# Token sets of 256 and 264 columns, side by side in PSUM, in a hybrid decoder layer

## The chip, the cores and the metric

The kernel runs on one core of a Trainium2 chip. The metric is the device time of one execution in microseconds (us). TensorE does the matrix products, VectorE and ScalarE the elementwise work, GpSimd a few set-up steps and the DMA requests for cached keys. PSUM, into which TensorE writes its products, has 8 banks; in this kernel it is the tensor `PS[128, 8, 512]` of float32, so a bank holds 512 columns.

## The reference

One layer of a decoder whose heads stand in parallel: eight attention heads with forget gates, and eight blocks of a gated linear recurrence. There are 512 new prompt tokens (one sequence) and 8 sample tokens, one for each of eight sequences with 2048 cached positions. All 520 tokens go through the same weights:

```
xn = rms_norm(x, g_mix)                       # 520 tokens x 2048
z  = xn @ w_in                                # q | k | v | forget | lru x | lru gate, 5 x 1024 + 8 columns
att = forgetting attention over z's q, k, v (prompt: causal; samples: 2048 cached rows + the new one)
lru = gelu(gate) * rg_lru(causal_conv(x-branch))
x  = x + concat(rms_norm(att), rms_norm(lru)) @ w_out         # 2048 x 2048
x  = x + square(relu(rms_norm(x, g_ffn) @ w_up)) @ w_down     # 2048 -> 8192 -> 2048
y  = rms_norm(x, g_final)
```

The new keys, values, forget logs, convolution rows and recurrent states are returned too. Everything is float32.

## The kernel before

**Layout.** Features lie on the 128 partitions and tokens along the free dimension: `A[128, 16, 520]` holds 16 feature tiles of all T = 520 tokens (512 prompt tokens, then the 8 samples).

**Precision.** TensorE's float32r form is the cheaper and the less exact of its two float forms. So each operand is split in a high and a low part (`XH`/`XL` or `HH`/`HL` for activations, `WH`/`WL` for weights), and each product is three: high x high, low x high, high x low. ScalarE makes the high parts of the weights and VectorE the low ones.

**Tiles.** A product tile is 128 output features x 520 tokens. 520 columns don't fit in a bank, so the tile takes a pair of banks and the tokens two sets, c = 0 and c = 1, with HT = T // 2 = 260 columns each. Bank 2p holds tokens 0 to 259 of pair p in its columns 0 to 259; bank 2p + 1 holds tokens 260 to 519 in its columns 0 to 259. The function `products` issues, for every contraction tile k, six matmuls: (xh, wh) for c = 0, 1, (xl, wh) for c = 0, 1, (xh, wl) for c = 0, 1. `pair_view(p)` is what other engines read of a pair: two runs of 260 columns, 512 apart.

**Stages around the change.** `unit` makes a tile of the input projection (16 k, 96 matmuls) and of the first hidden features. Units alternate between bank pairs 0 and 1 (`at`, `tile_wait`): while TensorE fills one pair, ScalarE or VectorE copies the other and then increments `tile_out`. Attention, recurrence, and the sums over cached values use banks 4 to 7 and are inserted between a unit's matmuls by hand (`insert`). `out_products` does the same for w_out with 8 k and 48 matmuls a tile. `down_tile` (4 k, 24 matmuls) makes the tiles of w_down; there the four pairs take turns, and `add_rows` on VectorE adds a finished pair to `A` and increments `d_out`.

**The up products** (`up_pair`, lines L2488 to L2490) work on one token half of 260 columns at a time, in a seven-product scheme whose operands are sums and differences of the two halves. They, the last four tiles of w_down in the last round (`split_products`), and the sums of squares (`norm_sums`) write columns 0 to 259 of single banks.

**Copies of one head.** For the keys and the values, `rows_out` copies tokens 0 to 259 (L947), tokens 260 to 511 (L948) and the 8 samples (L949) from three places; for the convolution input, L1002, L1003 and L1004 do the same. Other copies read `pair_view` in one instruction: L804, L848 and the gelu of L1025 on ScalarE, L1699 (`add_heads`), L1831 (`add_rows`) and L1905 (`scaled_tile`) on VectorE.

Of the kernel before, what the change touches and what calls it, by code (L numbers as in the profile page):

```python
# [9 lines left out]
ALU = mybir.AluOpType  # L10
ACT = mybir.ActivationFunctionType
# [8 lines left out]
def hymba_step(nc, x_prompt, x_sample, cache_k, cache_v, cache_logf, state_conv, state_h, page_table,  # L20
# [76 lines left out]
    with ExitStack() as ctx:  # L97
# [232 lines left out]
        def one(i):  # L330
            return bass.ds(i, 1)
# [88 lines left out]
        def pair_view(pair):  # L420

            return PS[:, 2 * pair:2 * pair + 2, 0:HT]
# [339 lines left out]
        def _(act):  # L762
# [33 lines left out]
            def lru_tile(u, m):  # L796

                k = out_tile(u, m)
                slot = tile_wait(U_O + 2 * u + m, 0)
                act.wait_ge(xl_ready, KD + (k + NH) % KD + 1)  # L800
                act.wait_ge(nsq_ready, (k + NH) % KD + 1)
                if k < NH:
                    act.wait_ge(queries_saved, 1)
                nc.scalar.activation(A[:, k, :].rearrange("p (c t) -> p c t", c=2), pair_view(slot), ACT.Copy)\  # L804
                    .then_inc(tile_out[slot], 1)
# [40 lines left out]
            def query_out(n, half, k):  # L846
                slot = tile_wait(n, half)
                nc.scalar.activation(A[:, one(k), :].rearrange("p a (c t) -> p (a c) t", c=2),  # L848
                                     pair_view(slot), ACT.Copy).then_inc(tile_out[slot], 1)
# [95 lines left out]
            def rows_out(full, dst, samples, i):  # L945

                nc.scalar.activation(dst[:, 0:HT], PS[:, 2 * full, 0:HT], ACT.Copy)  # L947
                nc.scalar.activation(dst[:, HT:SEQ], PS[:, 2 * full + 1, 0:HB], ACT.Copy)  # L948
                nc.scalar.activation(samples[:, one(i), :].rearrange("p a b -> p (a b)"), PS[:, 2 * full + 1, HB:HT], ACT.Copy)\  # L949
                    .then_inc(tile_out[full], 1)  # L950

            def step(i, head, prev, older=True, final=False):
# [44 lines left out]
                if head:  # L997
                    slot = tile_wait(U_L + 2, 2 * i)
                    if prev:
                        act.wait_ge(lru_done, i)  # L1000
                    W3 = CW - 1
                    nc.scalar.activation(XW[:, W3:W3 + HT], PS[:, 2 * slot, 0:HT], ACT.Copy)  # L1002
                    nc.scalar.activation(XW[:, W3 + HT:W3 + SEQ], PS[:, 2 * slot + 1, 0:HB], ACT.Copy)  # L1003
                    nc.scalar.activation(XW[:, W3 + SEQ:].rearrange("p (b j) -> p b j", j=CW)[:, :, W3],  # L1004
                                         PS[:, 2 * slot + 1, HB:HT], ACT.Copy).then_inc(tile_out[slot], 1)
# [19 lines left out]
                    nc.scalar.activation(PT[:, T:2 * T].rearrange("p (a t) -> p a t", a=2), pair_view(slot),  # L1025
                                         ACT.Gelu_apprx_tanh).then_inc(tile_out[slot], 1)
# [249 lines left out]
        def _(dve):  # L1276
# [418 lines left out]
            def add_heads(u):  # L1695

                for m, tmp_t in enumerate((TA, TB)):
                    slot = tile_wait(U_O + KD + 2 * u + m, 0)
                    V.tensor_tensor(tmp_t.rearrange("p (c t) -> p c t", c=2), pair_view(slot), RSA.rearrange("p (c t) -> p c t", c=2),  # L1699
                                    ALU.mult).then_inc(tile_out[slot], 1)  # L1700
# [202 lines left out]
            def scaled_tile(n):  # L1903
                slot = tile_wait(T_F + n, 0)
                V.scalar_tensor_tensor(hf[:, n, :].rearrange("p (a t) -> p a t", a=2), pair_view(slot), 0.0,  # L1905
                                       RS[:, :].rearrange("p (a t) -> p a t", a=2), ALU.max, ALU.mult).then_inc(tile_out[slot], 1)
# [107 lines left out]
        def _(pe):  # L2014
            mm = nc.tensor.matmul

            def products(xh, xl, wh, wl, dsts, kts, insert={}, first=True, last=True, ready=None):

                for n, k in enumerate(kts):
                    if ready and n in ready:
                        pe.wait_ge(*ready[n])
                    for x in (xh, xl):
                        for c in range(2):
                            mm(dsts[c], wh(k), x[:, k, c * HT:(c + 1) * HT], start=first and n == 0 and x is xh, stop=False)  # L2026
                    for f in insert.get(2 * n, ()):
# [8 lines left out]
            def unit(n, half, tile, tile_half, insert={}, kts=range(KD), first=True, last=True, ready=None, halves=False):  # L2036
# [11 lines left out]
                ins = products(XH, XL, lambda k: WH[slot][:, k * P:(k + 1) * P], lambda k: WL[slot][:, k * P:(k + 1) * P],  # L2048
                               [PS[:, 2 * pair + c, 0:HT] for c in range(2)], kts, insert, first, last, ready)
# [6 lines left out]
            def out_products(u, m, kts, insert={}, ready=None):  # L2056
# [4 lines left out]
                if kts[0] == k0:  # L2061
# [4 lines left out]
                               [PS[:, 2 * pair + c, 0:HT] for c in range(2)], kts, insert, kts[0] == k0, last, ready)  # L2066
# [426 lines left out]
            def down_tile(c, d, m, pair, kts, rows={}):  # L2493
# [3 lines left out]
                                [PS[:, 2 * pair + c2, 0:HT] for c2 in range(2)], kts, insert=rows, first=kts[0] == 0, last=kts[-1] == CF - 1)  # L2497
# [167 lines left out]
```

## Time and profile before

| | us |
|---|---|
| median of 3 runs | 2259.0 (2258.14 to 2259.13) |
| the profiled execution | 2259.51 |
| its span, first to last instruction | 2257.6 |
| TensorE busy | 2232.6 |
| VectorE busy | 1609.0 |
| ScalarE busy | 854.2 |
| GpSimd busy | 155.6 |

A matmul's duration in the profile (about 282 ns for 260 columns) runs from its start to its modelled end, and consecutive matmuls overlap; how much of TensorE a matmul takes is read from the distance between starts, or from the count in a stretch in which nothing else runs. The clock row gives TensorE's granted clock in tenths of full speed. TensorE's profile names a float32r product f32, and each float32 product shows as two instructions.

### The profile page before, as it was taken

The numbers are of one execution on the slowest core, as the hardware profiler recorded it, in microseconds if no ns is written. First come the engines' busy times: TensorE is split into PE (matmuls) and PEld (weight loads), VectorE is DVE, ScalarE is ACT, GpSimd is POOL, SyncE is SP. The second block draws the span as 40 slices with busy tenths as digits, with TensorE's granted clock in tenths as the row PEclk, the third lists the DMA queues.
The fourth block names the chain that finished last, engine by engine and source line by source line (L and its number), as shares of the span: only waits on it lengthen the run. The fifth ranks groups of instructions, "written<-read, shape, count | busy, mean of one in ns | idle before, by whom it ended". The sixth has DMA issues, their size and how long they took to land.

```text
span 2257.6 us, 50009 instructions
## 1 busy us (share of the span) xinstructions
PE 2232.6 (99%) x19862; PEld 2186.1 (97%) x19862; DVE 1609.0 (71%) x2064; ACT 854.2 (38%) x1210; POOL 155.6 (7%) x197
## 2 busy tenths in 40 slices
PE   7999999999999999999999999999999999999998
PEld 7999999999999999999999999999999999999997
DVE  7369999999974888767567567567566566576574
ACT  5224444334364334234234234233243243243245
POOL 0011111111113140000000000000000000000003
PEclk9999999999999999999999999999999999999999
DMA  7468999999965341433334334333333433433423
GB/s 241 112 192 280 336 334 334 346 327 324 331 212 207 113 137 57 122 103 113 112 102 121 111 103 121 98 116 108 106 115 100 120 111 87 136 99 97 135 81 112
DMA packets 387389, 367.50 MB, mean 163 GB/s; under 512 B 14339, under 2 KB 350628, under 8 KB 386644
## 3 DMA queue, kind: packets, MB, share of 16 engines
q1 hardware_dynamic: 357892, 293.28, 42.2%
q0 software_dynamic: 18608, 67.64, 8.2%
q10 hardware_dynamic: 10800, 5.31, 0.8%
q8 instruction: 66, 1.08, 0.2%
q14 instruction: 23, 0.19, 0.0%
HBM read 353.24 MB, written 12.94 MB: 162 GB/s over the span
## 4 chain that ended last, share of the span: by engine, by line
PE 92%; DVE 3%; ACT 1%; DMA 1%; issue 1%; DVEq 1%; SPq 0%; POOLq 0%; ACTq 0%
PE PS L2026 39%; PE PS L2030 19%; PE PS L2490 9%; PE PS L2489 9%; PE PS L2488 9%; PE PS L2206 2%; PE PS L2233 1%; PE PS L2254 1%; DMA KR<-in_cache_k 1%; DVE KR L1430 1%; PE PS L2396 1%; DVE WL L1283 1%; DMA RAW<-in_w_in 0%; PE PS L2244 0%; ACT WH L770 0%
## 5 line engine op out<-in xcount | busy, mean ns | idle before, releaser
L1123 ACT ACTIVATE WH<-RAW 128x1024 fp32r<-128x1024 f32 x293 | 304.9, 1056 | 679.2 <-PE PS L2030 521.2
L1728 DVE TENSOR_TENSOR WL<-RAW,WH 128x1024 fp32r<-128x1024 f32 x293 | 358.3, 1223 | 131.4 <-ACT WH L1123 130.0
L2026 PE MATMUL PS<-HH,WH 128*128 128x260 f32 x2016 | 406.0, 282 | 1.1 <-issue 0.6
L2030 PE MATMUL PS<-HH,WL 128*128 128x260 f32 x2016 | 404.9, 282 | 0.0
L2026 PE MATMUL PS<-HL,WH 128*128 128x260 f32 x2016 | 404.4, 282 | 0.0
L2026 PE MATMUL PS<-XH,WH 128*128 128x260 f32 x1920 | 396.7, 288 | 5.1 <-DVE XL L1352 5.0
L2030 PE MATMUL PS<-XH,WL 128*128 128x260 f32 x1920 | 386.9, 283 | 0.0
L2026 PE MATMUL PS<-XL,WH 128*128 128x260 f32 x1920 | 386.7, 283 | 0.0
L1831 DVE TENSOR_TENSOR A<-A,PS 128x520 f32<-128x520 f32 x252 | 174.9, 696 | 259.9 <-PE PS L2030 259.4
L2026 PEld LDWEIGHTS PS<-HH,WH 128*128 128x128 f32 x2016 | 309.7, 188 | 1.8 <-issue 1.1
L2026 PEld LDWEIGHTS PS<-HL,WH 128*128 128x128 f32 x2016 | 311.2, 188 | 0.0
L2030 PEld LDWEIGHTS PS<-HH,WL 128*128 128x128 f32 x2016 | 310.5, 188 | 0.0
L2026 PEld LDWEIGHTS PS<-XH,WH 128*128 128x128 f32 x1920 | 296.1, 189 | 14.3 <-issue 9.3
L2030 PEld LDWEIGHTS PS<-XH,WL 128*128 128x128 f32 x1920 | 296.6, 189 | 0.0
L2026 PEld LDWEIGHTS PS<-XL,WH 128*128 128x128 f32 x1920 | 296.3, 189 | 0.0
L2488 PE MATMUL PS<-XH,WH 128*128 128x260 f32 x960 | 271.6, 283 | 0.0
L2490 PE MATMUL PS<-XH,WL 128*128 128x260 f32 x960 | 271.0, 282 | 0.0
L2489 PE MATMUL PS<-XL,WH 128*128 128x260 f32 x960 | 270.9, 282 | 0.0
L2489 PE MATMUL PS<-TX,WH 128*128 128x260 f32 x720 | 203.4, 283 | 0.0
L2490 PE MATMUL PS<-TX,WL 128*128 128x260 f32 x720 | 203.3, 282 | 0.0
L2488 PE MATMUL PS<-TX,WH 128*128 128x260 f32 x720 | 202.4, 281 | 0.0
L1283 DVE TENSOR_TENSOR WL<-RAW,WH 128x2048 fp32r<-128x2048 f32 x59 | 135.0, 2288 | 86.2 <-ACT WH L770 86.1
(365 smaller groups left out, 3145.1 us busy)
## 6 DMA issues: line engine op xcount, KB each, us to landing
KR<-in_cache_k POOLq DMA_DIRECT2D x128, 512.0 KB, 6.1
VR<-in_cache_v SPq DMA_DIRECT2D x128, 512.0 KB, 5.9
RAW<-in_w_up SPq DMA_DIRECT2D x128, 512.0 KB, 4.2
RAW<-in_w_down SPq DMA_DIRECT2D x128, 512.0 KB, 4.5
RAW<-in_w_in SPq DMA_DIRECT2D x80, 512.0 KB, 7.9
RAW<-in_w_out SPq DMA_DIRECT2D x32, 512.0 KB, 5.8
TMP<-in_w_up SPq DMA_DIRECT2D x30, 512.0 KB, 6.2
xT_spill<-A SPq DMA_DIRECT2D x1, 4160.0 KB, 15.8
```

What stands on the lines that cost most here:

```text
L1123: nc.scalar.activation(RING_H[SLOT[i]], RB[b], ACT.Copy).then_inc(f_hi, 1)
L1283: V.tensor_tensor(WL[slot][:, :], RAW[:, slot, :], WH[slot][:, :].bitcast(F32), ALU.subtract)\
L1430: V.tensor_tensor(KR[:, b % NKS, :], KR[:, b % NKS, :], QB[:, :], ALU.mult).then_inc(dve_prod, 1)
L1728: V.tensor_tensor(RING_L[SLOT[i]], RB[op_block(i)], RING_H[SLOT[i]].bitcast(F32), ALU.subtract).then_inc(f_lo, 1)
L1831: V.tensor_tensor(rows, rows, pair_view(pair), ALU.add).then_inc(d_out[pair // 2], 1)
L2026: mm(dsts[c], wh(k), x[:, k, c * HT:(c + 1) * HT], start=first and n == 0 and x is xh, stop=False)
L2030: ins = mm(dsts[c], wl(k), xh[:, k, c * HT:(c + 1) * HT], start=False, stop=last and n == len(kts) - 1)
L2206: ins = mm(PS[VQ * m:VQ * m + 1, 7, half * HD:(half + 1) * HD], PP[:, n, b:b + 1], VR[:, b % NVS, n * HD:(n + 1) * HD], start=b == 0 and h ...
L2233: mm(dst, qcur[:, t * P:(t + 1) * P], kT[:, 0:n], start=True, stop=False)
L2488: mm(dst, wh[:, w], xh[:, k, :], start=q < 3 and k == 0, stop=False, skip_group_check=True)
L2489: mm(dst, wh[:, w], xl[:, k, :], start=False, stop=False, skip_group_check=True)
L2490: ins = mm(dst, wl[:, w], xh[:, k, :], start=False, stop=q in (3, 5, 6) and k == KB - 1, skip_group_check=True)
```

## The change

The tokens are now cut at 256 instead of 260 (`TOKENS`, which was already defined for other uses: columns 0 to 255 and 256 to 519). In the pair's first bank the 256 columns go to the bank's end (columns 256 to 511), and in the second bank the 264 columns begin at column 0, so that the 520 columns of a pair are one run of addresses across the bank border. `pair_view` is that run, `pair_banks` gives its two parts as matmul targets, and the three copies of `rows_out` and of the convolution input become two: 512 prompt columns, and the 8 samples. The scheme of `up_pair`, the split last tiles and the sums of squares keep their 260 columns and places.

```diff
-    HB = SEQ - HT
+    TA0 = SEQ // 2
...
         def pair_view(pair):
-            return PS[:, 2 * pair:2 * pair + 2, 0:HT]
+            first = 2 * pair * 512 + 512 - TA0
+            return PS[:, :, :].rearrange("p b n -> p (b n)")[:, first:first + T]
+
+        def pair_banks(pair):
+            return PS[:, 2 * pair, 512 - TA0:512], PS[:, 2 * pair + 1, 0:T - TA0]
...
             def rows_out(full, dst, samples, i):
-                nc.scalar.activation(dst[:, 0:HT], PS[:, 2 * full, 0:HT], ACT.Copy)
-                nc.scalar.activation(dst[:, HT:SEQ], PS[:, 2 * full + 1, 0:HB], ACT.Copy)
-                nc.scalar.activation(samples[:, one(i), :].rearrange("p a b -> p (a b)"), PS[:, 2 * full + 1, HB:HT], ACT.Copy)\
+                nc.scalar.activation(dst[:, 0:SEQ], pair_view(full)[:, 0:SEQ], ACT.Copy)
+                nc.scalar.activation(samples[:, one(i), :].rearrange("p a b -> p (a b)"), pair_view(full)[:, SEQ:T], ACT.Copy)\
                     .then_inc(tile_out[full], 1)
...
-                    nc.scalar.activation(XW[:, W3:W3 + HT], PS[:, 2 * slot, 0:HT], ACT.Copy)
-                    nc.scalar.activation(XW[:, W3 + HT:W3 + SEQ], PS[:, 2 * slot + 1, 0:HB], ACT.Copy)
+                    nc.scalar.activation(XW[:, W3:W3 + SEQ], pair_view(slot)[:, 0:SEQ], ACT.Copy)
...
-                rows = A[:, 2 * d + m, :].rearrange("p (a t) -> p a t", a=2)
+                rows = A[:, 2 * d + m, :]
                 V.tensor_tensor(rows, rows, pair_view(pair), ALU.add).then_inc(d_out[pair // 2], 1)
...
-            def products(xh, xl, wh, wl, dsts, kts, insert={}, first=True, last=True, ready=None):
+            def products(xh, xl, wh, wl, pair, kts, insert={}, first=True, last=True, ready=None):
+                dsts = pair_banks(pair)
                 for n, k in enumerate(kts):
...
                     for x in (xh, xl):
                         for c in range(2):
-                            mm(dsts[c], wh(k), x[:, k, c * HT:(c + 1) * HT], start=first and n == 0 and x is xh, stop=False)
+                            mm(dsts[c], wh(k), x[:, k, TOKENS[c]], start=first and n == 0 and x is xh, stop=False)
...
                     for c in range(2):
-                        ins = mm(dsts[c], wl(k), xh[:, k, c * HT:(c + 1) * HT], start=False, stop=last and n == len(kts) - 1)
+                        ins = mm(dsts[c], wl(k), xh[:, k, TOKENS[c]], start=False, stop=last and n == len(kts) - 1)
```

The other copies (L804, L848, L1025, L1699, L1905) lose their two-run form in the same way as L1831.

## Rows read from the trace of the kernel before

**Rows 1.** The page: engine shares, and the granted clock in 40 slices.

```profile
PE 2232.6 (99%) x19862; PEld 2186.1 (97%) x19862; DVE 1609.0 (71%) x2064; ACT 854.2 (38%) x1210; POOL 155.6 (7%) x197
...
PEclk9999999999999999999999999999999999999999
```

**Rows 2.** The page, the chain that ended last: shares by engine and by line.

```profile
PE 92%; DVE 3%; ACT 1%; DMA 1%; issue 1%; DVEq 1%; SPq 0%; POOLq 0%; ACTq 0%
PE PS L2026 39%; PE PS L2030 19%; PE PS L2490 9%; PE PS L2489 9%; PE PS L2488 9%; PE PS L2206 2%; PE PS L2233 1%; PE PS L2254 1%; DMA KR<-in_cache_k 1%; DVE KR L1430 1%; PE PS L2396 1%; DVE WL L1283 1%; DMA RAW<-in_w_in 0%; PE PS L2244 0%; 
```

**Rows 3.** Waits of TensorE: us in total, times, longest.

```profile
PE PS L2026 <- DVE XL L1352: 5.0, 2, 3.1
...
PE PS L2026 <- DVE A L1831: 0.2, 1, 0.2
```

**Rows 4.** Busy time by stretch; columns as the first line has them.

```profile
core 0: us, PE busy (x) PEld busy (x) DVE busy (x) ACT busy (x) POOL busy (x), PEclk, DMA share, GB/s
...
880.00:2190.00 1310.00, 1309.05 (x10930) 1308.55 (x10929) 868.00 (x1126) 460.30 (x614) 0.53 (x1) 1.00 0.37 110
```

**Rows 5.** Groups by line and form: name, form, count; busy us, mean ns; idle before.

```profile
L2026 PE MATMUL PS<-HH,WH 128*128 128x260 f32 x2016 | 406.0, 282 | 1.1 <-issue 0.6 <-DVE WL L1728 0.4 <-DVE A L1831 0.2
...
L2026 PE MATMUL PS<-XH,WH 128*128 128x260 f32 x1920 | 396.7, 288 | 5.1 <-DVE XL L1352 5.0
...
L2488 PE MATMUL PS<-XH,WH 128*128 128x260 f32 x960 | 271.6, 283 | 0.0
```

**Rows 6.** Timeline of TensorE in a projection unit: start us, us, what.

```profile
464.67 0.41 PE L2026 MATMUL PS<-XH,WH 128*128 128x260 f32 x2
...
465.40 0.40 PE L2026 MATMUL PS<-XH,WH 128*128 128x260 f32 x2
...
466.11 0.41 PE L2026 MATMUL PS<-XH,WH 128*128 128x260 f32 x2
```

**Rows 7.** Timeline of TensorE around two float32r products of 512 columns.

```profile
448.70 0.62 PE L2328 MATMUL PS<-QROW,SELQ 128*128 128x512 f32 x2
449.16 0.40 PE L2026 MATMUL PS<-XH,WH 128*128 128x260 f32 x2
```

**Rows 8.** Timeline of TensorE in one head's scores.

```profile
460.65 0.65 PE L2233 MATMUL PS<-kT,qcur 128*128 128x256 f32 x2
...
461.25 0.22 PE L2235 MATMUL PS<-maskneg,ident_r 128*128 128x128 f32 x1
...
462.25 1.07 PE L2233 MATMUL PS<-kT,qcur 128*128 128x512 f32 x2
...
463.38 0.22 PE L2235 MATMUL PS<-maskneg,ident_r 128*128 128x128 f32 x1
```

**Rows 9.** Groups by line and form, the weight loads.

```profile
L2026 PEld LDWEIGHTS PS<-HH,WH 128*128 128x128 f32 x2016 | 309.7, 188 | 1.8 <-issue 1.1 <-DVE WL L1728 0.6
```

**Rows 10.** Groups by line and form, VectorE.

```profile
L1831 DVE TENSOR_TENSOR A<-A,PS 128x520 f32<-128x520 f32 x252 | 174.9, 696 | 259.9 <-PE PS L2030 259.4
...
L1703 DVE TENSOR_TENSOR A<-A,KR 128x520 f32<-128x520 f32 x16 | 11.4, 711 | 1.8 <-issue 0.4
```

**Rows 11.** Groups by line and form, ScalarE, copies out of PSUM.

```profile
L804 ACT ACTIVATE A<-PS 128x520 f32<-128x520 f32 x16 | 9.6, 602 | 33.2 <-PE PS L2030 33.1
...
L958 ACT ACTIVATE QB<-PS 128x1024 f32<-128x1024 f32 x8 | 8.1, 1010 | 1.5 <-PE PS L2319 1.5
...
L1013 ACT ACTIVATE vtok<-PS 128x512 f32<-128x512 f32 x8 | 4.8, 600 | 4.7 <-ACT qcur L1013 4.7
...
L947 ACT ACTIVATE PR<-PS 128x260 f32<-128x260 f32 x8 | 3.2, 405 | 8.4 <-PE PS L2030 8.4
L1002 ACT ACTIVATE XW<-PS 128x260 f32<-128x260 f32 x8 | 3.1, 389 | 14.4 <-PE PS L2030 14.4
L947 ACT ACTIVATE kT<-PS 128x260 f32<-128x260 f32 x8 | 3.1, 384 | 10.0 <-PE PS L2235 10.0
L948 ACT ACTIVATE kT<-PS 128x252 f32<-128x252 f32 x8 | 3.0, 376 | 0.0
```

More of the change, by code:

```diff
@@ L803, in lru_tile @@
                     act.wait_ge(queries_saved, 1)
[L804 removed]
+                nc.scalar.activation(A[:, k, :], pair_view(slot), ACT.Copy)\
                     .then_inc(tile_out[slot], 1)
@@ L847, in query_out @@
                 slot = tile_wait(n, half)
-                nc.scalar.activation(A[:, one(k), :].rearrange("p a (c t) -> p (a c) t", c=2),
-                                     pair_view(slot), ACT.Copy).then_inc(tile_out[slot], 1)
+                nc.scalar.activation(A[:, one(k), :].rearrange("p a t -> p (a t)"), pair_view(slot), ACT.Copy)\
+                    .then_inc(tile_out[slot], 1)
             act.wait_ge(raw_full[0], 64)
@@ L1001, in step @@
                     W3 = CW - 1
-                    nc.scalar.activation(XW[:, W3:W3 + HT], PS[:, 2 * slot, 0:HT], ACT.Copy)
-                    nc.scalar.activation(XW[:, W3 + HT:W3 + SEQ], PS[:, 2 * slot + 1, 0:HB], ACT.Copy)
+                    nc.scalar.activation(XW[:, W3:W3 + SEQ], pair_view(slot)[:, 0:SEQ], ACT.Copy)
                     nc.scalar.activation(XW[:, W3 + SEQ:].rearrange("p (b j) -> p b j", j=CW)[:, :, W3],
-                                         PS[:, 2 * slot + 1, HB:HT], ACT.Copy).then_inc(tile_out[slot], 1)
+                                         pair_view(slot)[:, SEQ:T], ACT.Copy).then_inc(tile_out[slot], 1)
                     split_hi(U_L + 4, 2 * i)
@@ L1024, in step @@
                     slot = tile_wait(U_L + 3, 2 * i)
-                    nc.scalar.activation(PT[:, T:2 * T].rearrange("p (a t) -> p a t", a=2), pair_view(slot),
-                                         ACT.Gelu_apprx_tanh).then_inc(tile_out[slot], 1)
+                    nc.scalar.activation(PT[:, T:2 * T], pair_view(slot), ACT.Gelu_apprx_tanh).then_inc(tile_out[slot], 1)
             step(0, True, False, False)
@@ L1698, in add_heads @@
                     slot = tile_wait(U_O + KD + 2 * u + m, 0)
-                    V.tensor_tensor(tmp_t.rearrange("p (c t) -> p c t", c=2), pair_view(slot), RSA.rearrange("p (c t) -> p c t", c=2),
-                                    ALU.mult).then_inc(tile_out[slot], 1)
+                    V.tensor_tensor(tmp_t, pair_view(slot), RSA, ALU.mult).then_inc(tile_out[slot], 1)
                     dve.drain()
@@ L1904, in scaled_tile @@
                 slot = tile_wait(T_F + n, 0)
-                V.scalar_tensor_tensor(hf[:, n, :].rearrange("p (a t) -> p a t", a=2), pair_view(slot), 0.0,
-                                       RS[:, :].rearrange("p (a t) -> p a t", a=2), ALU.max, ALU.mult).then_inc(tile_out[slot], 1)
+                V.scalar_tensor_tensor(hf[:, n, :], pair_view(slot), 0.0, RS[:, :], ALU.max, ALU.mult).then_inc(tile_out[slot], 1)
             def tile_lo(n):
@@ L2048, in unit @@
                 ins = products(XH, XL, lambda k: WH[slot][:, k * P:(k + 1) * P], lambda k: WL[slot][:, k * P:(k + 1) * P],
-                               [PS[:, 2 * pair + c, 0:HT] for c in range(2)], kts, insert, first, last, ready)
+                               pair, kts, insert, first, last, ready)
                 if last:
@@ L2065, in out_products @@
                                lambda k: WL[slot][:, (2 * (k - k0) + m) * P:(2 * (k - k0) + m + 1) * P],
-                               [PS[:, 2 * pair + c, 0:HT] for c in range(2)], kts, insert, kts[0] == k0, last, ready)
+                               pair, kts, insert, kts[0] == k0, last, ready)
                 if last:
@@ L2496, in down_tile @@
                 return products(HH, HL, lambda k: wh[:, (2 * k + m) * P:(2 * k + m + 1) * P], lambda k: wl[:, (2 * k + m) * P:(2 * k + m + 1) * P],
-                                [PS[:, 2 * pair + c2, 0:HT] for c2 in range(2)], kts, insert=rows, first=kts[0] == 0, last=kts[-1] == CF - 1)
+                                pair, kts, insert=rows, first=kts[0] == 0, last=kts[-1] == CF - 1)
             def hidden_wait(c, k):
```

## The prediction

> **What bounds the kernel now.** I read the engine shares first: TensorE is busy for 99% of the span and has its full granted clock in every slice of the page [rows 1]. Then the chain that ended last: 92% of it is TensorE, and lines L2026 and L2030, the three products of a tile that the change touches, are 39% and 19% [rows 2]. Then the waits of TensorE itself: the largest is 5.0 us in two waits for VectorE's low part of x, and for `add_rows`, the step that frees a bank pair, it waited once, 0.2 us [rows 3]. Nobody delays TensorE, so the kernel's time is the number of matmuls times the distance of their starts, plus small products and the ends. In the 1310 us of the feed-forward stage 10,930 matmuls start, 1310 / 10,930 = 119.85 ns each [rows 4]. At 2.4 GHz, the level of a granted clock of 1.00, 260 columns would be 108.3 ns; 11.5 ns more are spent.
>
> **TensorE's part of the change.** Six groups of matmuls change: three with HH or HL, 2016 each, and three with XH or XL, 1920 each; the first of either three stands in [rows 5]. Together 3 x (2016 + 1920) = 11,808, or 5904 pairs (c = 0 and c = 1) with the same weights. At 119.85 ns they take 1415 us, 63% of the span. The 5040 up products (3 x 960 with X, of which one row is shown [rows 5], and 3 x 720 with TX) keep 260 columns. No matmul and no weight load goes or comes; a pair has 520 columns before and after. What may change is what a pair costs: 2 x 119.85 = 239.7 ns for 260 + 260, and the trace has no 256 + 264.
>
> Is the cost linear in columns? Two float32r products of 512 columns start within 449.16 - 448.70 = 0.46 us [rows 7], 230 ns each. From 260 to 512 columns that is 110 ns for 252 columns, 0.437 ns a column. By this line 256 columns cost 119.85 - 1.75 = 118.1 ns and 264 cost 121.6 ns, again 239.7 in all. The scores let me look below 260: from the start of the key product with n columns (float32) to the mask product, with a float32r product of n columns between, it is 0.60 us for n = 256 (461.25 - 460.65) and 1.13 us for n = 512 (463.38 - 462.25) [rows 8]. The 0.53 us for 256 columns more are 2.07 ns a column, or 0.414 ns in each of five passes, if the float32 product is taken as four. That is again the clock's 1 / 2.4 ns, and the point at 256 is on no step. So my value for the term is 0 us.
>
> Its bounds come from another fact. Six matmuls of one k take 0.73 us (464.67 to 465.40), and the next six, same length, 0.71 us (465.40 to 466.11) [rows 6]: 121.7 and 118.3 ns a matmul. What differs between them is where their operands lie. The new cut changes the second set's start from column 260 to 256 and its place in PSUM, so the cost may move in this band. If all 11,808 went like the faster six, it would be 11,808 x 1.55 = 18 us less, if all like the slower, 11,808 x 1.85 = 22 us more. But the mean 119.85 is over starts of both sets and all k, and only one set of the two gets a new start, so half of each end, -9 and +11 us, is what I carry to the range.
>
> **ScalarE's part.** Each head had three copies of 512 tokens in two pieces: for keys 384 + 376 ns, for values 405 + about 408, for the convolution 389 + 376 [rows 11]; the partners of L947's second form and of L1002 measure like the shown 252-column copy within 32 ns. One piece of 512 columns out of PSUM took 600 ns [rows 11], so some 160, 210 and 165 ns go, 0.54 us a head, 4.3 us over eight heads. A run across a bank border is already in this kernel: QB, 1024 columns from two adjoining banks, took 1010 ns [rows 11], 1010 - 600 = 410 ns for 512 columns more or 0.80 ns each, so the border costs nothing that shows. The whole-pair copies (L804, 602 ns for 520 in two runs [rows 11]) lie on the same line as the 600 for 512 in one run: nothing to gain there. ScalarE is busy for 38% of the span, and before L804 it is idle for 33.2 us waiting for TensorE [rows 1, 11]. The 4.3 us are saved under TensorE's work: 0 us on the path. What is late next is again TensorE.
>
> **VectorE's part.** `add_rows` reads two runs of 260 and takes 696 ns; an addition of 520 columns in one run, all in SBUF, takes 711 [rows 10]. So the two-run form costs nothing that could be saved; I bound the change by 15 ns either way, 252 x 0.015 = 3.8 us of an engine that before these very instructions is idle for 259.4 us waiting for TensorE [rows 10]. If the cover were gone, all 3.8 us would count, but a down tile is 24 x 119.85 ns = 2.88 us and its pair is refilled four tiles after its last filling, so the addition has three tiles, 8.6 us, for 0.7 us. In the projections the copy has one unit, 96 matmuls or 11.5 us. No wait is added, no step moves past a queue, no DMA changes.
>
> **Sum.** TensorE 0, ScalarE 0, VectorE 0. The profiled execution is 2259.51 us (span 2257.6 and 1.9 around it), 0.5 us above the median of the runs. I forecast the median unchanged: 2259.0 us.
>
> **Rivals.**
>
> *The weight load holds up the shorter matmul (slower).* Every matmul brings its own load of 128 columns, 188 ns in the profile [rows 9], and loads run for 97% of the span [rows 1], under the matmul ahead. If the distance of 119.85 ns is set by the load and the matmul together so that 260 columns lie just at the corner, 256 columns gain nothing, and 264 cost 4 x 0.437 = 1.75 ns more. It decides from 260 columns upward. Price: 5904 x 1.75 = 10.3 us, so 2269 us. For it: the 11.5 ns beyond 108.3. Against it: 512 columns have such an excess too, 230 - 213.3 = 17 ns, where a load has twice the time to hide. If the load alone set the pace well above 264 columns, nothing would change at all, which is my forecast again. The Trainium skill (TensorE: Matmul & The Clock Gate, LDWEIGHTS) gives a load as its columns over 1.2, an estimate of 107 ns here; by that rule and the same page's gap of columns / 2.4 + 2.5 the load is below 109 ns for 256 columns, no corner is reached, and the sum stays 0; the trace does not show a load's time by itself.
>
> *Whole pieces (faster).* If TensorE fetched the moving tokens in pieces of 8 columns, 260 would be 33 pieces (264 columns), 256 would be 32 and 264 be 33: a pair would save 8 columns, 8 / 2.4 = 3.3 ns, in all 5904 x 3.3 = 19.7 us, 2239 us. With pieces of 16 columns (17 + 17 against 16 + 17) it is 6.7 ns and 39 us, 2220 us. For it: the excess over 108.3, and the band between places [rows 6]. Against it: an excess of the same kind at 512, a whole number of any such pieces [rows 7]. The Trainium skill (SBUF — State Buffer, Specifications) has lines of 16 bytes, four float32: 260 would be 65 whole lines, 256 + 264 be 130, and by that rule the sum is 0; the rows don't show a line's size.
>
> *The places in memory, without a rule (either side).* The band above, at half its width: 2250 to 2270 us.
>
> *The change does less than it says.* Copies as one run may be no faster at all. That would cost ScalarE's 4.3 us, and the time is the same: part of the forecast.
>
> **Chances.** What a measurement of this kernel can tell from no change is about 0.2%, 4.5 us. Forecast (within 4.5 us): 0.62. Weight-load corner: 0.12, all slower. Whole pieces: 0.07, all faster. Places: 0.19, of which 0.10 faster and 0.09 slower. So faster 0.17, same 0.62, slower 0.21. The range leaves out the whole pieces and a little on each side: 2248 to 2270 us.
>
> **What would show it.** In the changed kernel's page TensorE should again be busy for 99%, with 19,862 matmuls; the feed-forward stretch should again give 119.85 ns a matmul, 239.7 for a pair, with the mean of the up products unchanged. ScalarE should be some 4 us less busy, its 512-column copies at 600 ns and L1831 at 690 to 710 ns. TensorE should still wait for `add_rows` under 1 us. I am wrong if the pair's distance moves by more than 0.8 ns (5904 x 0.8 = 4.7 us), if the granted clock of the page falls, or if TensorE begins to wait for `tile_out` or `d_out`.

## The result: 0.14% slower, and the profile after

The changed kernel takes 2262.5 us in the median of 22 runs, the kernel before 2259.5; the ratio is 1.0014, with a 95% interval of 1.0008 to 1.0020. It is a small loss, but a clear one. One execution of the kernel before took 4430.2 us and doesn't count in the ratio; its others took 2258.1 to 2261.6 us. The profiled execution of the changed kernel has a span of 2261.4 us against 2257.6, 3.7 us more by the unrounded spans. The page of the changed kernel, engine shares and chain:

```profile
PE 2238.6 (99%) x19862; PEld 2192.3 (97%) x19862; DVE 1609.4 (71%) x2064; ACT 854.3 (38%) x1186; POOL 155.5 (7%) x197
...
PEclk9999999999999999999999999999999999999999
...
PE 96%; DVE 2%; ACT 1%; DMA 0%; DVEq 0%; issue 0%; ACTq 0%; SPq 0%
```

As many matmuls, the same digits for the granted clock, VectorE and GpSimd alike; TensorE is busy 6.0 us longer (2232.6 before, [rows 1]), 2.0 us of them in the first 36 us of the span. Its own waits in the changed kernel (us in total, times, longest):

```profile
PE PS L2025 <- DVE XL L1354: 4.0, 2, 2.1
...
PE PS L2025 <- DVE A L1832: 0.2, 1, 0.2
```

They correspond to 5.0 and 0.2 us in [rows 3]: no wait has been added. So the time lies in the distances of the matmuls. The feed-forward stage of the changed kernel, same stretch and columns as [rows 4]:

```profile
880.00:2190.00 1310.00, 1309.59 (x10916) 1309.27 (x10915) 867.88 (x1123) 459.79 (x610) 0.00 (x0) 1.00 0.37 109
```

10,916 matmuls in place of 10,930: 120.01 ns each in place of 119.85. In a projection unit, every sixth matmul of the changed kernel's timeline (start us, us, what):

```profile
465.49 0.40 PE L2025 MATMUL PS<-XH,WH 128*128 128x256 f32 x2
...
466.20 0.40 PE L2025 MATMUL PS<-XH,WH 128*128 128x256 f32 x2
...
466.92 0.40 PE L2025 MATMUL PS<-XH,WH 128*128 128x256 f32 x2
...
467.65 0.40 PE L2025 MATMUL PS<-XH,WH 128*128 128x256 f32 x2
```

0.71, 0.72 and 0.73 us for six matmuls, in the band of [rows 6]. Steps of ten nanoseconds don't resolve a change of half a nanosecond a pair, so from here on I use the start times of all 19,862 matmuls in a trace. For each changed matmul I take the distance to the next start, leave out distances over 190 ns (other work stands between), and average: separately in the down tiles (HH, HL) and in the tiles of XH and XL, and by length. A pair is the sum of its two averages.

| | down tiles, pair | XH/XL tiles, pair | up products, one |
|---|---|---|---|
| before, 260 + 260 | 2 x 119.53 = 239.1 ns | 2 x 119.97 = 239.9 | 119.96 |
| changed, 256 + 264 | 118.87 + 120.99 = 239.9 | 118.49 + 121.76 = 240.3 | 119.97 |

All time between two changed matmuls in a row adds up to 721.9 us in the down tiles before and 724.3 after, and to 693.4 and 695.0 in the XH/XL tiles, 4.0 us in all, beside the 3.7 that the span grew. Some 0.7 of the 4.0 us are not the change's: they are distances over 190 ns near the start of the span, most of them where the granted clock is still 0.50, and that stretch ends later in the profiled execution of the changed kernel. The line from 34 to 36 us, first of the kernel before, then of the changed one (columns as in [rows 4]):

```profile
34.00:36.00 2.00, 2.00 (x18) 2.00 (x17) 1.93 (x4) 1.10 (x2) 0.00 (x0) 0.93 1.10 471
34.00:36.00 2.00, 2.00 (x11) 2.00 (x11) 1.97 (x3) 1.18 (x2) 0.00 (x0) 0.50 0.84 361
```

The distances in the table alone give 3024 x 0.8 + 2880 x 0.3 = 3.3 us, which fits the 3.0 us between the medians. Nothing else is needed to explain the loss. The rest of this document asks why a pair of the same 520 columns costs more.

ScalarE and VectorE of the changed kernel, groups by line and form, as in [rows 10, 11]:

```profile
L952 ACT ACTIVATE PR<-PS 128x512 f32<-128x512 f32 x8 | 4.9, 617 | 8.4 <-PE PS L2029 8.4
...
L1006 ACT ACTIVATE XW<-PS 128x512 f32<-128x512 f32 x8 | 4.8, 602 | 14.6 <-PE PS L2029 14.6
...
L952 ACT ACTIVATE kT<-PS 128x512 f32<-128x512 f32 x8 | 4.8, 595 | 10.0 <-PE PS L2234 10.0
```

```profile
L1832 DVE TENSOR_TENSOR A<-A,PS 128x520 f32<-128x520 f32 x252 | 175.1, 696 | 262.6 <-PE PS L2029 261.2
```

The merged copies take 595 to 617 ns, as expected, and the addition 696 ns, as before. Yet ScalarE is busy for 854.3 us, where it was 854.2. The two pieces of a key copy in the kernel before overlapped, as the view of tile kT shows (durations min/median/max, first and last start):

```profile
L947 ACT ACTIVATE kT<-PS x8: 363/387/389, 147.9 to 593.9; 128x260 f32<-128x260 f32 x8
L948 ACT ACTIVATE kT<-PS x8: 371/377/377, 148.2 to 594.2; 128x252 f32<-128x252 f32 x8
```

The second starts 0.3 us after the first, which takes 0.39. Together they kept ScalarE for some 0.68 us, not 0.76, and one copy of 0.60 saves about half of what the sum of durations promised. Counted over all copies of these lines, the samples' included, ScalarE was occupied for 17.7 us before and 16.2 after: 1.5 us saved. Even that doesn't show in the page's total, where other ScalarE groups differ by some tenths of a microsecond and the changed kernel's trace has two more records of a weight copy, `WH<-RAW` of 1024 columns (295 against 293). None of it is on the path.

### The profile page after: what moved, and what is told of

Same layout as the page of the kernel before. It is cut to its first block, busy times and chain, and to the rows that moved or that the text cites. A ratio compares the mean times of both kernels' runs of the same rounds, so it can differ in the third digit from the quotient of the medians.

```text
span 2261.4 us, 49985 instructions
## 1 busy us (share of the span) xinstructions
PE 2238.6 (99%) x19862; PEld 2192.3 (97%) x19862; DVE 1609.4 (71%) x2064; ACT 854.3 (38%) x1186; POOL 155.5 (7%) x197
## 4 chain that ended last, share of the span: by engine, by line
PE 96%; DVE 2%; ACT 1%; DMA 0%; DVEq 0%; issue 0%; ACTq 0%; SPq 0%
PE PS L2025 41%; PE PS L2029 20%; PE PS L2489 9%; PE PS L2488 9%; PE PS L2487 9%; PE PS L2205 3%; PE PS L2232 1%; PE PS L2253 1%; PE PS L2395 1%; DVE WL L1285 0%; PE PS L2243 0%; DMA XT<-in_x_prompt 0%; ACT WH L775 0%; DVE A L1322 0%; PE PS L2106 0%; PE PS L2543 0%
## 5 line engine op out<-in xcount | busy, mean ns | idle before, releaser
L2025 PE MATMUL PS<-HL,WH 128*128 128x256 f32 x2016 | 407.6, 284 | 0.0
L2025 PE MATMUL PS<-HH,WH 128*128 128x256 f32 x2016 | 405.0, 282 | 1.1 <-issue 0.6
L2029 PE MATMUL PS<-HH,WL 128*128 128x256 f32 x2016 | 405.8, 282 | 0.0
L2025 PE MATMUL PS<-XH,WH 128*128 128x256 f32 (+1 forms) x1920 | 397.1, 288 | 4.1 <-DVE XL L1354 4.0
L2029 PE MATMUL PS<-XH,WL 128*128 128x256 f32 (+1 forms) x1920 | 388.1, 283 | 0.0
L2025 PE MATMUL PS<-XL,WH 128*128 128x256 f32 (+1 forms) x1920 | 388.0, 283 | 0.0
L2029 PEld LDWEIGHTS PS<-HH,WL 128*128 128x128 f32 x2016 | 315.1, 189 | 0.0
L2487 PE MATMUL PS<-XH,WH 128*128 128x260 f32 x960 | 271.6, 283 | 0.0
L2489 PE MATMUL PS<-XH,WL 128*128 128x260 f32 x960 | 270.9, 282 | 0.0
L2488 PE MATMUL PS<-XL,WH 128*128 128x260 f32 x960 | 270.9, 282 | 0.0
```

The lines of the kernel that those rows point to most:

```text
L2025: mm(dsts[c], wh(k), x[:, k, TOKENS[c]], start=first and n == 0 and x is xh, stop=False)
L2029: ins = mm(dsts[c], wl(k), xh[:, k, TOKENS[c]], start=False, stop=last and n == len(kts) - 1)
L2487: mm(dst, wh[:, w], xh[:, k, :], start=q < 3 and k == 0, stop=False, skip_group_check=True)
L2488: mm(dst, wh[:, w], xl[:, k, :], start=False, stop=False, skip_group_check=True)
L2489: ins = mm(dst, wl[:, w], xh[:, k, :], start=False, stop=q in (3, 5, 6) and k == KB - 1, skip_group_check=True)
```

## The experiments

There are three theories at first: S, that the distance of matmuls depends on where their tokens lie in SBUF; P, that the new place in PSUM costs; W, that a weight load is a floor under the shorter matmul.

**1. The cut alone.**

```diff
-    mm(dsts[c], wh(k), x[:, k, c * HT:(c + 1) * HT], ...)
+    mm(dsts[c], wh(k), x[:, k, TOKENS[c]], ...)            # 256 and 264, each from column 0 of its bank
```

> The kernel before with one part of the change: the token sets are cut at 256 (256 and 264 columns), but each set still begins at column 0 of its bank, and the copies are the old ones of two runs of 260. (The tokens from 256 on so end up four places off in the copies; this run is read for its time alone.) The changed kernel took 3.0 us more than the one before (2262.5 against 2259.5), all of it seen as a longer distance between matmuls, about 0.5 ns a pair. Theory S (SBUF places: the distance of two matmuls depends on where their moving tokens start in SBUF): the cut makes the loss, so this run is as slow as the changed kernel, ratio 1.001 to 1.002, and the median distances at each place in a down tile are those of the changed kernel. Theory P (PSUM places: writing at a bank's columns 256 to 511, next to the other bank's start, makes it): this run is at 1.000 with the same distances as before. Theory W (the weight load is a floor under the shorter matmul): ratio 1.001 to 1.002 as in S; the next run with a cut of 240 parts S and W.

Measured: 2262.0 us, ratio 1.0012 (1.0003 to 1.0021). The pairs are 239.9 and 240.3 ns, and the median distances at the 24 places of a down tile are those of the changed kernel, at most 0.5 ns apart. P falls: the cut makes the loss without any change in PSUM.

**2. The place in PSUM and the one-run copies alone.**

```diff
-    TA0 = SEQ // 2
+    TA0 = 260                                             # and the sets are cut at TA0
```

> The changed kernel with the cut put back to 260 and 260 columns: the two sets still adjoin in PSUM (columns 252 to 511 of the one bank and 0 to 259 of the next), and the copies still read one run. Theory S: back to the time before, ratio 1.000 (0.999 to 1.0005), and the median distances in a down tile are those of before, place by place. Theory P: 1.001 to 1.002, distances as in the changed kernel. Theory W: 1.000.

Measured: 2259.7 us, ratio 1.0001 (0.9992 to 1.0010). The feed-forward stretch of this run has exactly the count of [rows 4]:

```profile
880.00:2190.00 1310.00, 1309.05 (x10930) 1308.55 (x10929) 867.70 (x1126) 460.98 (x615) 0.53 (x1) 1.00 0.37 110
```

The distances are those of before at each place. Adjoining sets and one-run copies cost nothing and bring nothing that shows.

**3. A cut at 240.** The same with `TA0 = 240`.

> The changed kernel with the cut at 240 (240 and 280 columns, still adjoining, still one run). Theory W: the set of 240 columns is 20 columns below the corner and gains nothing, the set of 280 pays 20 x 0.437 = 8.7 ns; 5904 pairs make 52 us, so about 2311 us. Theory S: the sum of a pair stays at 239 to 241 ns, 2255 to 2267 us, and the distance after a matmul of 240 columns is about 111 ns, after one of 280 about 129 ns.

Measured: 2270.8 us, ratio 1.0051 (1.0037 to 1.0064). 240 columns take 111.0 ns, so no weight load holds the shorter matmul up near the 118 to 120 ns of this kernel, and W falls. But 280 take 130.6, so the pair is at 241.6 ns in the down tiles and 241.3 in the others, 1.4 to 2.6 more than before, which S had not said.

**4. Everything shifted.** The kernel before, and:

```diff
+    sb("PAD", [P, 4], scope=x_scope)                      # ahead of XH
```

> The kernel before, unchanged but for four unused float32 columns (16 bytes) allocated ahead of XH, so that the tokens' high and low parts lie 16 bytes further on in SBUF, while the weights stay. No instruction is added or removed. Theory S: the distances of the matmuls at each place in a tile change by some ns, and the time moves by 1 to 10 us one way or the other (ratio outside 0.9996 to 1.0004). Theories P and W: no change, ratio 1.000, and the same distances as before at every place.

Measured: 2260.6 us, ratio 1.0004 (0.9995 to 1.0014), which alone tells nothing. The distances tell: in the XH/XL tiles the six medians at k0 were 118, 121, 114, 124, 118, 120 ns and are now 119, 123, 120, 117, 122, 118, which before were those of k1; k1 now has those of k2, and so on around. Sums over the six matmuls of a k, ns:

```
                    k0   k1   k2   k3   k4   k5   k6   k7
XH/XL, before      715  719  717  741  723  719  720  711
XH/XL, shifted     719  717  741  723   ...
down, before       707  719  716  725   (2867)
down, shifted      714  719  726  723   (2882)
```

The pattern repeats after eight k (k8 to k15 like k0 to k7), and eight rows of tokens are 16,640 bytes = 65 x 256. So the place within 256 bytes sets the distances; the 16 bytes must have been rounded up to 32, the step from one k to the next (2080 = 8 x 256 + 32). An XH/XL tile goes through all eight places, and its mean stays at 119.97. A down tile has k0 to k3 alone, four of the eight: it lost 15 ns a tile. The up products gained, 119.96 to 119.63.

**5. The changed kernel shifted by 32 bytes.**

> The changed kernel with 32 unused bytes ahead of XH, nothing else. The 16 bytes asked for in the run before this one moved the pattern of median distances by exactly one k (k0 then had the values that k1 had, and so on), and k's tokens lie 2080 bytes after those of k - 1, which is 8 x 256 + 32; so the place in a stretch of 256 bytes seems to decide, and the 16 had been rounded up to 32. Theory S: the same here: in the tiles of XH and XL the sums over six matmuls, 720, 721, 716, 727, 716, 721, 725, 724 ns for k0 to k7 in the changed kernel, become 721, 716, 727, 716, 721, 725, 724, 720, with the same mean; in a down tile 726, 717, 717, 723 become 717, 717, 723 and one new value; the time lies 0.5 to 3 us below or above that of the changed kernel. Theory P or W: the pattern does not move and the time is the changed kernel's, 2262.5 us.

Measured: 2264.7 us, ratio 1.0021 (1.0012 to 1.0031). The XH/XL pattern moved by one k as said, same mean (240.3 a pair). The down tiles went to 720, 721, 723, 730: only partly what was said. Matmul for matmul, k2 now has the medians that k3 had, k1 has those of k2 in all but the first and the third of six, and k0 does not have those of k1. In experiment 4 too only k2 took over the medians of the next k (within 1 ns); k0 and k1 did not. A down tile begins right after the k3 of the tile before it, so what goes ahead of a matmul seems to count beside its own place; no run tests that. A pair is 240.7, another 0.9 more.

Set beside experiment 4, this run says something of the cut itself. With 32 bytes of shift 260 + 260 takes 239.9 ns a pair in the down tiles and 256 + 264 takes 240.7; without a shift it was 239.1 and 239.9. In the XH/XL tiles, whose mean is over all eight places, it is 240.0 and 240.3 with the shift, 239.9 and 240.3 without. So the cut at 256 costs the same 0.8 and 0.3 ns at either place (ratios 1.0004 and 1.0021 with the shift), and the loss is not the luck of one place.

**6. Only HH and HL shifted, by 128 bytes.**

```diff
+    sb("PADF", [P, 32], scope=ffn_scope)                  # ahead of HHF, and the same ahead of HH
```

> The kernel before (260 + 260, sets at column 0) with 128 unused bytes ahead of HH, so that only the operands of the down tiles move, by half of 256 bytes. Theory S: only the distances in down tiles change: the sums per k, 707, 719, 716, 725 ns (2867 together), become those of the other four places; over eight places the tiles of XH and XL add up to 5765, so I expect 5765 - 2867 = 2898 here, 31 ns a tile more, 252 tiles: 7.8 us slower, about 2267 us; the up products stay at 119.96 ns. Were place of no matter, 2259.5 us.

Measured: 2262.5 us, ratio 1.0013 (1.0003 to 1.0023): as large a loss as the change's, without the change. The sums are 718, 722, 721, 719 = 2880, a pair 240.0; the XH/XL tiles have not moved. The size of 31 ns a tile was wrong (13 measured): the XH/XL sum is no guide to that of HH and HL. One more thing follows: of the three places tried for 260 + 260 in the down tiles, two take 239.9 to 240.0 ns a pair, and the kernel before has the third, 239.1.

**7. A cut at 200.**

> The changed kernel with the cut at 200 (200 and 320 columns). At 240 + 280 a pair took 241.6 ns, the shorter matmul 111.0 (11.0 over columns / 2.4), the longer 130.6 (13.9 over), and the kernel 11.2 us more. Theory L (what a matmul takes over columns / 2.4 is about 11 up to some length between 264 and 280 columns and about 14 above it): 200 columns take 94.3, 320 take 147.3, the pair 241.6 again, and the time is that of the cut at 240, 2270 to 2272 us. Theory G (the excess grows steadily with the difference of the two): 25 ns over for the longer, more than 2300 us. Theory W (a floor under short ones): 200 columns take about 111 ns or more, 2350 us.

Measured: 2368.6 us, ratio 1.0481 (1.0464 to 1.0499). Timeline of TensorE in a down tile of this run, two matmuls (200 and 320 columns) a row:

```profile
1499.87 0.42 PE L2027 MATMUL PS<-HH,WH 128*128 128x200 f32 x2
1500.13 0.42 PE L2027 MATMUL PS<-HL,WH 128*128 128x200 f32 x2
1500.39 0.42 PE L2031 MATMUL PS<-HH,WL 128*128 128x200 f32 x2
```

0.26 us a pair: 92.1 ns for 200 columns and 166.2 for 320. L falls, W falls as stated, and G in its shape: the excess doesn't grow steadily, it is 2.6 ns a pair at a difference of 40 and 19 at 120. TensorE's waits are as before here too.

The trace shows where the 19 ns lie. Here are the weight loads around the 320-column matmul that starts at 1500.22 (the next one, of 200 columns, starts at 1500.39):

```profile
1500.14 0.19 PEld L2027 LDWEIGHTS PS<-HL,WH 128*128 128x128 f32 x1
1500.24 0.19 PEld L2031 LDWEIGHTS PS<-HH,WL 128*128 128x128 f32 x1
1500.39 0.19 PEld L2031 LDWEIGHTS PS<-HH,WL 128*128 128x128 f32 x1
1500.50 0.19 PEld L2027 LDWEIGHTS PS<-HH,WH 128*128 128x128 f32 x1
```

In the other runs read for this (the kernel before, the changed one, and 240 + 280, 252 + 268, 256 + 256 and 320 + 320) a load starts about 3 ns after the matmul ahead of it has started. Here that holds for the loads behind a 200 (3.2 ns in the mean), but those behind a 320 start 19.5 ns after it. Nearly all of them (5526 of 5763) start 108 or 109 ns after the load before them, and from 900 us on no two such loads start less than 108 ns apart in any of this case's 20 traces, even where matmuls start 92 ns apart. From such a late load to the next matmul it is 146.6 ns, hardly more than the 144 ns of 320 beside 320. So some 16.5 of the 19 ns are a load that comes late, because the one before it started only 108 ns ago. That is a form of W that takes hold where a matmul takes less than 108 ns, by the line of the prediction under an estimated 233 columns. It is read from the trace; no run moves the loads by themselves. At 240 + 280 no load is late (3.0 ns), so the 1.4 to 2.6 ns there are something else, and 2.6 ns remain here too.

**8. 260 + 260 adjoining, with both shifts.**

> 260 + 260 columns that adjoin in PSUM with the one-run copies, XH, XL and TX moved by 32 bytes, and HH and HL by 32 + 224 = 256 bytes. Theory S with a period of 256 bytes: the down tiles have the distances of before place by place (119.53 ns in the mean), the tiles of XH and XL stay at 119.94, and the up products keep the gain that the run with 16 bytes showed, 119.96 to 119.63 ns over 5040 matmuls, 1.7 us: 2257.8 us, ratio 0.9990 to 0.9997, faster than both kernels. If the period is longer than 256, the down tiles change too, by an unknown amount of at most 8 us.

Measured: 2258.6 us, ratio 0.9995 (0.9986 to 1.0005). The down tiles have the distances of before at every place, with 256 bytes of shift: the period is 256. The up products are at 119.68. Of the 1.7 us expected, 1.2 show, and the interval holds 1.000 too: no gain is shown.

**9 to 12. Starts and lengths apart.** The kernel before with other slices, for instance:

```diff
-    mm(dsts[c], wh(k), x[:, k, c * HT:(c + 1) * HT], ...)
+    mm(dsts[c], wh(k), x[:, k, 256 * c:256 * c + 260], ...)
```

> The kernel before, but the second set's 260 columns are read from token 256 on instead of 260 (the last four tokens get no product, 256 to 259 get theirs twice; read for its time alone). So both sets keep their length and the second one has the start of the changed kernel. Over all runs so far the cut of 256 + 264 costs the same beside 260 + 260 whatever shift both have: 0.8 ns a pair in the down tiles (239.06 to 239.86, and 239.94 to 240.74 with 32 bytes of shift), 0.3 ns in the tiles of XH and XL (239.9 to 240.2). Theory A (the second set's start makes it): pair 239.9 in the down tiles and 240.2 in the others, the places' pattern that of the changed kernel, about 2262 us, ratio 1.001 to 1.0015. Theory B (the two lengths make it): 239.1 and 239.9 ns and the pattern of before, 2259.5 us, ratio 1.000.

Measured: 2281.7 us, ratio 1.0096 (1.0082 to 1.0110). Neither: the pairs are 244.1 and 242.8 ns. The feed-forward stretch:

```profile
880.00:2190.00 1310.00, 1309.75 (x10813) 1309.53 (x10813) 858.12 (x1115) 451.17 (x596) 0.00 (x0) 1.00 0.37 108
```

117 matmuls fewer than in [rows 4]. The instructions and lengths are the same; one start of two is 16 bytes earlier, tokens 256 to 259 are read by both sets, and the kernel is 22 us longer.

> Both sets have 264 columns, starts as in the changed kernel (0 and 256), so eight tokens are multiplied twice. Linear cost (0.437 ns a column): 121.6 ns a matmul, 243.2 a pair, 5904 pairs x 3.5 = 21 us more than before, 2280 us. If the longer matmul of an uneven pair pays for being beside a shorter one, this even pair is below 2 x the distance after a 264 in the changed kernel, which was 121.0 in the down tiles and 121.7 in the others.

Measured: 2294.2 us, ratio 1.0153 (1.0137 to 1.0169). 122.8 ns a matmul in both kinds of tile, 245.6 a pair: 2.4 above the line. It is not below 2 x 121.0 or 2 x 121.7, so the 264 of the changed kernel doesn't pay for its shorter neighbour.

> Both sets have 256 columns, starts 0 and 256; eight tokens get no product. Linear: 118.1 ns a matmul, 236.2 a pair, 5904 x 3.5 = 21 us less, 2238.5 us. If 256 columns in an uneven pair lost something to their longer neighbour, the even pair is below 2 x 118.9 (down tiles) and 2 x 118.5 (others).

Measured: 2245.6 us, ratio 0.9938 (0.9922 to 0.9954). 118.3 and 118.0 ns a matmul, 236.6 and 235.9 a pair: on the line of the prediction (118.1). The starts are those of the run with 260 + 260 from 0 and 256, which took 244.1: four columns less in each set take off 7.5 ns a pair, where the line says 3.5. So a start at token 256 isn't dear by itself.

> Both sets have 320 columns, starts 0 and 200 as with the cut at 200, where a matmul of 320 columns took 166.5 ns (33 over its 133.3 at the clock) and one of 200 took 91.9 (8.6 over). Theory L (length alone: a matmul over some 300 columns takes 33 ns over): 166 ns each, 11,808 x 46.6 = 550 us more, about 2810 us. Theory U (unevenness: the pair waits for something that even matmuls hide): 133.3 + 11 to 15, about 146 ns each, 11,808 x 26.5 = 313 us more, about 2570 us. By the line of the prediction it would be 119.85 + 60 x 0.437 = 146 ns.

Measured: 2575.9 us, ratio 1.1398 (1.1379 to 1.1416). 146.9 and 146.7 ns a matmul. U holds, and the line nearly (146). The 166 ns of experiment 7 belong to the uneven pair, not to 320 columns; what most of it goes to is the late load shown there.

**13 to 16. Gap, overlap and two more cuts.** C says that a second set which doesn't begin where the first ended costs 3 to 5 ns; P2, that the second start's place in 32 bytes decides.

> The kernel before with the first set cut short: 256 columns from token 0, 260 from token 260, so the second set keeps its start and its length, and four tokens between get no product. Theory P2 (the place of the second start decides, the first set costs its length): a pair costs that of before less 4 x 0.437 = 1.75 ns: 237.3 ns in the down tiles, 238.1 in the others, about 2249 us. Theory C (a second set that does not begin where the first ended costs 3 to 5 ns a pair): 241 to 243 ns, 2270 to 2275 us.

Measured: 2254.9 us, ratio 0.9980 (0.9971 to 0.9990), pairs 238.7 and 238.2. C falls for gaps; P2 is met in the XH/XL tiles and missed by 1.4 ns in the down tiles.

> The changed kernel with the cut at 264 (264 and 256 columns, still adjoining and contiguous; the second set starts 1056 bytes in, 33 x 32, as 1024 is 32 x 32). Theory C: as the changed kernel, 239.5 to 240.5 ns a pair, 2259 to 2264 us. Theory P2: the second set again starts on a whole 32 bytes, with a shorter length behind it: 239 to 244 ns. A run under 2258 us would say that the order long, short is the better one.

Measured: 2262.9 us, ratio 1.0016 (1.0006 to 1.0025), pairs 240.0 and 240.2. Both theories allow it, and long before short is not the better order.

> The changed kernel with the cut at 252 (252 and 268 columns, contiguous; the second set starts 1008 bytes in, 16 past a whole 32, as with 260). Theory C: 239.5 to 240.5 ns a pair, 2259 to 2264 us. Theory P2: the second start is of the good kind, so 239.1 and 239.9 ns as before, 2259.5 us. Theory U (unevenness costs: 0.5 ns at a difference of 8, 1.8 at 40, 19 at 120): 240.0 to 240.7 ns, 2260 to 2265 us.

Measured: 2262.4 us, ratio 1.0010 (1.0001 to 1.0020), pairs 240.3 and 239.1. P2 is missed by 1.2 ns in the down tiles, and the XH/XL pair lies below what C and U said. It is the dearest of these cuts in the down tiles and the cheapest in the others.

> 260 columns from token 0 and 260 from token 252, an overlap of 8 (the last eight tokens get no product). The second start lies 16 bytes past a whole 32, as in the kernel before. Theory P2: the pair of before, 239.1 and 239.9 ns, 2259.5 us. Theory C: 242.8 to 244.1 ns as with the start at 256, about 2281 us.

Measured: 2268.6 us, ratio 1.0040 (1.0026 to 1.0054), pairs 240.7 and 241.4. Both miss. No rule in bytes of 32 fits: starts at 252, 256 and 260 with 260 columns take 240.7, 244.1 and 239.1 ns in the down tiles.

**17, 18. Each cut where it is cheap.**

```diff
-    TA0 = SEQ // 2
+    CUT_X, CUT_H = 252, 260
...
-                dsts = pair_banks(pair)
+                cut = CUT_H if xh is HH else CUT_X
+                sets = (slice(0, cut), slice(cut, T))
+                dsts = pair_banks(pair, cut)
```

> Adjoining sets and one-run copies everywhere; cut at 252 in the tiles of XH and XL, at 260 in the down tiles. If costs add: 2892 pairs x (239.94 - 239.12) = 2.4 us less than before, the rest as before: 2257.2 us, ratio 0.9987 to 0.9992, the median distances in the down tiles those of before, place by place. If the gain at 252 belonged to something else in that run: 2259.5 us.

Measured: 2257.3 us, kernel before 2259.2 on the same chip, ratio 0.9991 (0.9982 to 1.0000). The down tiles have the distances of before, the XH/XL pair 239.05. The costs add.

> The same with XH, XL and TX moved by 32 bytes and HH and HL by 256. If costs add: another 5040 x (119.96 - 119.66) = 1.5 us less: 2255.7 us, ratio 0.9980 to 0.9986, clearly faster than the kernel before (2259.5) and the changed one (2262.5). If place effects of the one stage carry over into another: anything between 2255 and 2262 us.

Measured: 2257.1 us, ratio 0.9990 (0.9981 to 0.9999). The up products do get cheaper (119.68), but the time stays that of the run before. In the two profiled executions, from start to next start, the up products save 1.5 us, the XH/XL matmuls take 1.35 more and the down tiles 0.3 more, though their distances under 190 ns hardly move (by 0.1 ns a pair); why is open. Both are faster than the changed kernel (2262.5 in its own runs), and the last is also just faster than the one before.

## Why the prediction was wrong

**TensorE's term: the step that failed.** The prediction put it at 0, because two lengths, 260 and 512, lay on a line and 256 on no step. The line itself is met by 256 + 256, which take 118.0 to 118.3 ns a matmul (118.1 by the line), and nearly by 320 + 320 with 146.7 to 146.9 (146 by it); 264 + 264 take 122.8 and not 121.6. What failed is the use of a line for a difference of half a nanosecond. Around it a pair of 520 columns with sets of 252 to 268 took anything from 239.1 to 244.1 ns, by starts and cut. The change took 0.8 ns a pair more in the down tiles and 0.3 in the others, 3.3 us by these distances and 3.0 in the medians, where I had said 0. I had also set what can be told from no change at 4.5 us, or 0.8 ns a pair, by which this result would pass for none; with 22 executions of either kernel the interval reaches 1.4 us to each side, and the 3.0 us lie outside it.

**The band of places: the right mechanism, but not carried to its end.** The prediction saw that the same six matmuls take 0.71 or 0.73 us by place [rows 6] and made that a rival on either side. It then halved the ends because the mean was over all k. That holds for the XH/XL tiles, which go through all eight places in 256 bytes: a shift leaves their mean unchanged. A down tile goes through four and averages over half of them only: a shift of 32 or 128 bytes alone costs its pairs 0.9 ns. That much was readable before: from the start times of a tile's matmuls, k by k, and from the 2080 bytes between two k. That the kernel before stood at the cheapest of the three places tried was not readable: the XH/XL pattern said 31 ns a tile for 128 bytes, and 13 were measured. Nor does the place alone explain the loss. The cut costs 0.8 ns at both places at which it was tried, and 0.3 ns in the XH/XL tiles, which have every place; of the sets that adjoin, the cut at 256 costs these tiles 240.3 ns a pair, 264 takes 240.2, 260 takes 239.9 and 252 takes 239.1. What counts is how the two starts and lengths go together, and in no run is that reduced to a rule.

**The weight-load corner: wrong at 260 columns.** 240 columns take 111.0 ns, the line's value, in experiment 3, and 200 take 92.1 in experiment 7, so 260 lie at no corner. A limit by the loads exists, but lower: they start at least 108 ns apart, which is nothing to matmuls of 118 to 122 ns and some 16.5 ns a pair to the cut at 200. The prediction said that the trace doesn't show a load's time by itself; where matmuls are short, the distance between load starts does show how soon one can follow another.

**Whole pieces: wrong.** 256 columns save 1.2 to 2.0 ns against 260 in an even pair, less than the 3.3 or 6.7 ns that a piece of 8 or 16 columns would save. And 264 columns, which would be as many such pieces as 260, take 122.8 ns and not 119.5 to 120.0.

**ScalarE and VectorE: 0 on the path, right.** The copies take 595 to 617 ns (600 said) and no wait arose. But the saving in ScalarE's busy time, 4.3 us, was a sum of durations that overlap in the profile; the copies save 1.5 us, and the page's total shows none of it.

**PSUM: right.** A run across the bank border costs nothing that shows, in reading, and neither do matmuls that write up to the border and on from it (experiment 2).

**What stays open.** Why a place is cheap, and why the cut at 256 costs 0.8 and 0.3 ns wherever it was put. The trace gives a period of 256 bytes and, for each start, a fixed pattern; it gives no rule from which a new cut's cost could be worked out, and three rules that I tried (contiguous sets, the place within 32 bytes, unevenness alone) each missed one run at least. In the runs with 260 columns from token 252 or 256 the start and the overlap of the two sets come together, and no run parts them. Open too are the 1.4 to 2.6 ns of the cut at 240, where no load is late.

## What to carry to other kernels

When TensorE is busy for 99% of a span and a change leaves the count of its matmuls and their columns in all alone, the time still moves by where the operands lie and how they are cut: here by 0.1% in versions that do the same work, and by 1% when one of two sets of 260 columns began 16 bytes earlier and overlapped the other. Before explaining a result of that size by the edit's purpose, shift an operand by 32 bytes in both kernels and compare them again at the same shift: a shift alone moved either kernel by 1 to 3 us, and a difference that a shift takes away is not the edit's. This one stayed. Keep both sets of a pair long enough that no matmul takes less than the 108 ns between two weight loads, and add up durations of neighbouring copies only after looking at their start times.

## What the runs showed of the hardware

- The distance of float32r matmuls of 260 columns is fixed by place, not random: at each of 24 places in a down tile of the kernel before 86 to 100% of the 242 tiles that nothing interrupts lie within 2 ns of their median, while the medians of the places go from 115 to 127 ns. It follows the moving operand's address with a period of 256 bytes (experiments 4, 5, 6, 8), and what goes ahead seems to count too (experiment 5). It is the same in tiles of 48 and 96 matmuls, whose weights lie elsewhere, though always a multiple of 512 bytes from the start of their buffer.
- 260 columns read 16 bytes earlier in one set of two, so that four tokens are read twice: 244.1 ns a pair in place of 239.1, 22 us. With 256 + 256 from the same starts the pair takes 236.6, on the line.
- Weight loads of 128 columns start at least 108 ns apart, at granted clock 1.00, in all 20 traces (from 900 us on), and 108 or 109 ns apart at 96% of the loads behind a 320 in 200 + 320 (experiment 7); matmuls themselves can start 92 ns apart.
- 200 beside 320 columns: 258.3 ns a pair, the 320 at 166.2; 320 beside 320: 146.9 each, so the even pair pays 13.6 ns a matmul over columns / 2.4 and the longer of the uneven pair 33, of which some 16.5 ns are the late load.
